# A two-layer trunk of attention and expert mixing on one core: other weight strips are kept on chip

## What is computed

```python
for layer in range(DEPTH):
    hn = rms_norm(h, ln_mix[layer])
    mix = gla_mixer(...) if layer % 2 == 0 else swa_mixer(...)   # linear attention / window of 128
    h = h + mix
    h = h + peer_ffn(rms_norm(h, ln_ffn[layer]), ...)
# peer_ffn, for each token: 8 heads, each picks 16 of 16384 experts
q = (xb @ w_q).reshape(BLK, PEER_HEADS, PEER_QDIM)      # scores against two sets of 128 keys
...
ue = u[e]                                                # e: top 16 of each set, top 16 of their sums
ve = v[e]
a = gelu(einsum('thkd,td->thk', ue, xb)) * g
return einsum('thk,thkd->td', a, ve)
```

## Time and profile before

| | |
|---|---|
| median of 3 runs | 2906.79 us (2900.58 to 2907.41) |
| the profiled execution | 2907.78 us, its span 2906.0 us |
| TensorE, VectorE, ScalarE, GpSimd busy | 78%, 75%, 41%, 43% of the span |
| mean granted TensorE clock | 0.921 |
| bytes moved by DMA | 1170.26 MB, 403 GB/s over the span |

### The profile page before, as it was taken

One profiled execution on the slowest core, in us unless ns is written; L12 is line 12 of the kernel. 1 busy time (PEld: TensorE's weight loads), 2 busy tenths in 40 slices (PEclk: granted clock), 3 DMA queues, 4 the chain that ended last, 5 costly groups with the idle time before them and its releaser, 6 DMA issues.

```text
span 2906.0 us, 27009 instructions
## 1 busy us (share of the span) xinstructions
PE 2257.9 (78%) x7300; PEld 1200.6 (41%) x7300; DVE 2185.6 (75%) x5166; ACT 1183.3 (41%) x3457; POOL 1263.8 (43%) x1049
## 2 busy tenths in 40 slices
PE   8678777687877877787787878878778777876667
PEld 6535443354423544243343434433444434432222
DVE  2687768875878757796688876988679876887664
ACT  2144324343443433344444463445534453433333
POOL 0155335443454433444434543354434454345555
PEclk9799899999998998899898998999899998998989
DMA  6499999999999999999999999999999999999998
GB/s 270 174 410 421 413 359 420 421 420 413 404 420 422 420 389 415 421 422 421 421 391 416 422 421 421 388 413 421 421 418 398 420 421 420 404 420 422 421 422 351
DMA packets 170816, 1170.26 MB, mean 403 GB/s; under 512 B 19668, under 2 KB 19928, under 8 KB 36136
## 3 DMA queue, kind: packets, MB, share of 16 engines
q0 software_dynamic: 147456, 1073.81, 89.4%
q1 hardware_dynamic: 23208, 94.74, 8.3%
HBM read 1164.28 MB, written 4.19 MB: 402 GB/s over the span
## 4 chain that ended last, share of the span: by engine, by line
DMA 29%; DVE 14%; PE 10%; issue 6%; POOL 3%; ACT 3%; POOLq 0%; DVEq 0%; ACTq 0%
DMA ring<-in_uv,pick 27%; PE acc L1716 5%; DVE ring L1093 5%; POOL ring L666 3%; PE ps L1511 3%; DVE side L1084 1%; DMA xc<-h 1%; DMA stream<-in_strips 1%; ACT diag L1369 1%; DVE arena L968 1%; DVE arena L949 1%; DVE arena L950 1%; ACT coef L1361 1%; DVE arena L1039 1%; DVE arena L1043 1%
## 5 line engine op out<-in xcount | busy, mean ns | idle before, releaser
L666 POOL DMA_INDIRECT ring<-in_uv,pick x1024 | 1259.3, 1230 | 1616.5 <-PE acc L1716 1084.1
L1716 PE MATMUL acc<-ring,diag 128*128 128x512 f32 x2988 | 1523.6, 652 | 474.6 <-ACT diag L1369 474.1
L1093 DVE CUSTOM_DVE_ANT_0 ring<-ring,h_now 128x1024 f32<-128x1024 f32 x1024 | 1236.0, 1223 | 494.5 <-DMA ring<-in_uv,pick 483.2
L1716 PEld LDWEIGHTS acc<-ring,diag 128*128 128x128 f32 x2988 | 576.0, 204 | 1286.0 <-ACT diag L1369 719.4
L1358 ACT ACTIVATE gelu<-dots 128x1 f32<-128x1 f32 x1024 | 206.1, 201 | 1263.2 <-DVE dots L1093 1261.8
L1084 DVE SCALAR_TENSOR_TENSOR side<-ring,coef,side 128x1024 f32<-128x1024 f32 x270 | 346.1, 1282 | 18.9 <-ACT coef L1361 18.9
L1361 ACT ACTIVATE coef<-gate,gelu 128x1 f32<-128x1 f32 x1024 | 301.9, 295 | 33.2
L1369 ACT ACTIVATE diag<-ident,coef 128x128 f32<-128x128 f32 x747 | 300.1, 402 | 28.2 <-PE acc L1716 3.9
L1511 PE MATMUL ps<-resident,actT 128*128 128x256 f32 x896 | 217.5, 399 | 16.5 <-ACT actT L1170 16.5
L1511 PEld LDWEIGHTS ps<-resident,actT 128*128 128x128 f32 x896 | 175.7, 200 | 59.4 <-ACT actT L1170 18.1
L1478 PE MATMUL ps<-actT,stream 128*128 128x128 f32 x960 | 125.6, 292 | 27.4 <-DMA stream<-in_strips 26.6
(11 more groups left out here) (196 smaller groups left out, 1439.2 us busy)
## 6 DMA issues: line engine op xcount, KB each, us to landing
stream<-in_strips SPq DMA_DIRECT2D x102, 512.0 KB, 9.3
resident<-in_strips SPq DMA_DIRECT2D x18, 1024.0 KB, 12.3
ring<-in_uv,pick POOLq DMA_INDIRECT x1024, 14.9
ring<-in_strips SPq DMA_DIRECT2D x9, 1024.0 KB, 19.7
arena<-in_keys SPq DMA_DIRECT2D x8, 512.0 KB, 7.8
xc<-in_x SPq DMA_DIRECT2D x4, 512.0 KB, 6.2
h<-arena SPq DMA_DIRECT2D x4, 512.0 KB, 11.5
xc<-h SPq DMA_DIRECT2D x4, 512.0 KB, 7.8
```

The source lines that it names most:

```text
L666: pool.indirect_dma_start(ring[:, n % SLOTS, :], None, tables[layer], bass.IndirectOffsetOnAxis(ap=pick[:, col:col + 1], axis=0),).then_in ...
L1093: dve.tensor_tensor_reduce(ring[:, slot, 0:D], ring[:, slot, 0:D], h_now[:], 1.0, 0.0, ALU.mult, ALU.add, dots[:, slot:slot + 1]).then_inc ...
L1716: m = pe.matmul(acc[:, b * 512:(b + 1) * 512], diag[:, turn % 4, :], ring[:, slot, D + b * 512:D + (b + 1) * 512], start=(r == 0 and i == ...
```

## The change

The nine kept strips are no longer the first nine of a layer. In layer 0 strips 5, 7, 9, 11, 13, 15, 16, 17, 18 are kept and 0 to 4, 6, 8, 10, 12, 14, 19 streamed; in layer 1 only 0, 4, 5 and 12 are streamed. Their number is as before. `left` now waits for the halves of its strip and says when it is done with them. q1, k0 and k1 of stage 0 stand at beats 41, 45 and 49. SP's queue is reordered to fit: the gain before strip 14 (layer 0) or 12 (layer 1), the keys behind all streamed strips, the rest of layer 1's kept strips behind three streamed ones, four kept strips loaded ahead in stage 2, not five. In the opening strips are loaded in the order of their numbers (14 and 19 last) into ring or `resident`, and all ring slots are free before the first gather, so that its wait for one goes.

```diff
-STREAMED = tuple(s - RESIDENT for s in STRIPS)
+KEPT = ((5, 7, 9, 11, 13, 15, 16, 17, 18), (1, 2, 3, 6, 7, 8, 9, 10, 11))
+PASSING = tuple(tuple(n for n in range(STRIPS[layer]) if n not in KEPT[layer]) for layer in range(2))
+STREAMED = tuple(len(p) for p in PASSING)
...
-SAYS = ({11: "r", 15: "y", 16: "pq0", 17: "pq1", 18: "pq2", 19: "pq3"},
-        {8: "y", 9: "pq0", 10: "pq1", 11: "pq2", 12: "pq3"})
-DONE = [[SAYS[layer].get(n) for n in range(RESIDENT, STRIPS[layer])] for layer in range(2)]
+SAYS = ({1: "q", 3: "k", 19: "pq3"}, {4: "kv", 12: "pq3"})
+DONE = [[SAYS[layer].get(n) for n in PASSING[layer]] for layer in range(2)]
 FREED = [[e for event in events for e in [None] * (CUTS - 1) + [event]] for events in DONE]
-GAIN_AT = (13 - RESIDENT, 10 - RESIDENT)
-AHEAD, AHEAD_AT, REST_AT = 5, 10, 5
-KEYS_AT = (16 - RESIDENT, 10 - RESIDENT)
+GAIN_AT = (PASSING[0].index(14), PASSING[1].index(12))
+AHEAD, AHEAD_AT, REST_AT = 4, 10, 5
...
-        "pe": {"hT": 34, "q0": 37, "q1": 39, "k0": 43, "k1": 46, "v0": 54, "v1": 54, "v2": 60, "v3": 60, "attn": 61,
+        "pe": {"hT": 34, "q0": 37, "q1": 41, "k0": 45, "k1": 49, "v0": 54, "v1": 54, "v2": 60, "v3": 60, "attn": 61,
...
             def load_kept_ahead(prep):
 
-                said_by(sp, "pe", before(prep), "v")
+                said_by(sp, "pe", before(prep), "r")
...
             def load_streamed(prep):
-                if prep.layer == 1:
-
-                    said_by(sp, "pe", prep, "o3")
-                    sp.dma_start(bias_out, b_out).then_inc(bias_loaded, 16)
                 opening = prep.first and prep.layer == 0
...
                 for n in range(STREAMED[prep.layer]):
-                    if n == GAIN_AT[prep.layer]:
+                    if n == GAIN_AT[prep.layer] + opening:
+
+                        if prep.layer == 1:
+                            if prep.first:
+                                load_kept_rest(prep)
+
+                            said_by(sp, "pe", prep, "o3")
+                            sp.dma_start(bias_out, b_out).then_inc(bias_loaded, 16)
 
                         said_by(sp, "pe", prep, "oT")
                         if prep.layer == 0:
 
                             said_by(sp, "dve", prep, "state1")
                         sp.dma_start(ffn_gain, gain_ffn[prep.layer:prep.layer + 1, :]).then_inc(gain_loaded, 16)
-                    if n == KEYS_AT[prep.layer]:
-
-                        said_by(sp, "pe", prep, "y")
-                        sp.dma_start(keysT, (keys0, keys1)[prep.layer]).then_inc(keys_loaded, 16)
...
+                said_by(sp, "pe", prep, "y")
+                sp.dma_start(keysT, (keys0, keys1)[prep.layer]).then_inc(keys_loaded, 16)
+
             def preps(prep, after):
-                if prep.first:
-                    load_kept_rest(prep)
                 load_streamed(prep)
...
+            def load_opening(begin, end):
+                for n in range(begin, end):
+                    if n in KEPT[0]:
+                        load_kept(Prep("gla", 0), KEPT[0].index(n))
+                    elif n in PASSING[0][:SLOTS]:
+                        i = PASSING[0].index(n)
+                        sp.dma_start(ring[:, i, :], strips[0][n]).then_inc(ring_loaded[i], 16)
...
-                    elif SAYS[0].get(RESIDENT + n, "r") not in ("r", "y", "pq0"):
-
-                        said_by(pool, "pe", Prep("gla", 0), SAYS[0][RESIDENT + n])
-                        alone(pool, passed["pool"])
...
-            def cut_done(n, c, ins):
-
-                if n >= RESIDENT and c < CUTS - 1:
+            def cut_done(prep, n, c, ins):
+
+                if passing(prep, n) and (c < CUTS - 1 or n not in SAYS[prep.layer]):
                     used_up(ins)
...
+                        if c == 0 and k % CUT == 0:
+                            cut_loaded(prep, n, k // CUT)
                         i = pe.matmul(ps[:, bank, (2 * side + c) * P:(2 * side + c + 1) * P],
                                       w[:, k, c * P:(c + 1) * P], actT[:, k, :], start=(k == 0),
                                       stop=(k == KT - 1))
+                        if c == 1 and k % CUT == CUT - 1:
+                            cut_done(prep, n, k // CUT, i)
```

42 lines of the change are left out of this document (19 added, 23 removed).

## The result

The changed kernel takes 2925.98 us (median; 2924.08 to 2929.37 over 4 runs), the kernel before 2906.26 beside it on the same chip. The ratio is 1.0069, 95% interval 1.0056 to 1.0083: slower by 20 us. The forecast was 2885 us with a range from 2870 to 2905, so the direction was wrong and the time lies outside the range. The profiled execution has a span of 2924.7 us.

What follows compares the result with a forecast made beforehand. DMA was taken as the bound wherever its ring is fed, at 421 GB/s. The sum was 2907.8 - 18.5 - 6 + 1 = 2884.3 us profiled, 2883.3 against the median, stated as 2885, range 2870 to 2905.

Steps and rivals of the forecast that it cites:

- Bytes: Whole kernel: as many strips streamed and kept per block as before, the 1170 MB unchanged, so 0 us.
- The pq strips of swa: Swa preparations: streaming only pq3 removes a 3.1 us wait at pq1; half taken, 1.5 a stage, 6 us won.
- Out and pq strips of gla: Gla preparations: all stream waits at out and pq go, winning 9.8 + 3.3 + 5.4 = 18.5 us of 22.1.
- Hand-overs of q and k: New streamed strips: 13 us each, leaving TensorE 2 us short in stage 0, inside the cover; 1 us lost.
- the slower rival: Hand-over of a q or k strip takes 17 us, not 13, deciding from about 15.5: 2915 us; chance 0.08.
- The 9.5: Stage 0: three beats and 2 us of waits put alpha 9.5 us later; VectorE may stand 0 to 2 us.
- the room of (b + 1) x 2.49: DMA time a hand-over b beats ahead has: b gathers and the strip itself, 2.49 us each.
- The rival on the clock: Stage 0: new waits drop TensorE's clock, 2.9 us more at each of seven hand-overs: 2895 us; chance 0.05.
- SP's queue, opening, stage starts: Reordered queue waits and loads, opening loads and the strip loaded at stage starts: 0 us each, opening at best 2.5.
- A rule beside the rows: DMA engines alternate between queues packet by packet, so a half strip takes 2.5 us; the sum used 11.3 us hand-overs instead.
- The signs: Right: stream waits gone at out and pq, DMA above 410 GB/s at 340 to 440 us; wrong: longer alpha wait.

Runs made afterwards that it cites:

- before's two profiles: The unchanged kernel before, profiled a first and a second time: gla loss 23.3 and 27.3 us, swa loss 18.8 and 20.6; the second execution took 2912.28 us.
- the mixed kernels: Three kernels against the kernel before: layer 1's strips as before, layer 0's exchanged so no two q or k strips stream consecutively; 2902.21, 2901.77 and 2902.42 us.

## Why the prediction was wrong

**The step that failed is "Bytes": "Nothing is added to or taken from the 1170 MB: 0 us."** The megabytes were the same, but three strips a swa stage were moved out of room that DMA had anyway, to places where it has none. That costs what the room held: swa loss 18.8 to 46.4, time +19 to +20, and it comes back when strips are put behind pq0 again (10 us for the first). I had the row in hand: the prediction says that VectorE is busy 36.1 of 40 us in the swa dips and that "most of these dips are top-k work", and concluded only that nothing is won there. If VectorE sets the pace in a dip, then what streams in it is free, and taking it away can't shorten the dip.

**The pq strips of swa, -6: wrong in sign.** The waits at pq1 did go. But they lay in a stretch whose length was VectorE's, so their removal gave nothing, and the dips grew by 28 us, nearly the strips' own 30.

**Out and pq strips of gla, -18.5: a third came.** (One reading behind it was wrong: of the four out strips of stage 2 only out1 and out3 start after a wait on the stream; out0 and out2 start with none, and out2 waits only for its second half.) The waits on the stream are gone, and VectorE's 15.0 us for y in stage 0 became 3.3, as forecast. Stage 2, forecast 5.4, gave 6.2 (6.7 to 0.5). Stage 1, forecast 3.3, gave 0.5 (4.7 to 4.2). Stage 0, forecast 9.8, gave nothing (11.9 to 12.6). Altogether 6 of loss, and against before's two profiles 6 to 10; in time layer 0's change alone is 0 within 3 us.

**Hand-overs of q and k, 13 us each: mis-sized.** Three of the four take 15.4 to 15.9 and one 11.5, 58.3 us together where 3 x 12.45 and, for v0 at five beats, 14.9 are room for 52.3: a lag of 6.0 us, not 2. (The prediction counted v0's hand-over as tight too; with 14.9 us for it, the slower rival's lag at 17 us each is 15.7, not 18.) The average of 14.6 lies below the 15.5 from which the slower rival was to decide. It seems to have decided stage 0 all the same, though not as told: DMA stayed at 419 in 220 to 280 us, alpha came 20.6 us later (275.4 for 254.8) instead of 9.5, and most of the loss came after 340. The 9.5 left out a term: three strips now stream between q0 and k1, 7.5 us of DMA time that the room of (b + 1) x 2.49 counts and alpha's sum did not; with three beats (7.5) that leaves 5.6 for waits. Strips kept between them bring stage 0 to 6.3 to 7.7 us, and the time to 2902. The slower rival had the sign with this mechanism, 2915; but the slower result is layer 1's, which no rival named.

**The rival on the clock** was right in its mechanism: among the new waits the granted clock is 0.83 for 0.93; what that cost by itself no run shows. **SP's queue, opening, stage starts, 0:** the mixed kernels load strips in the opening and at the stage starts in this order, with the gain before strip 14, and are not slower. The keys behind all streamed strips and four strips ahead for five they don't share: the first is in the kernel with layer 0 alone (2905.4), the second only in kernels with layer 1's change, and no run took either singly in layer 0. The opening's loss (to 165 us) is 69.0 for 70.5.

**"A rule beside the rows"**: the turns between queues, by which a half strip would take an estimated 2.5 us (the Trainium skill, DMA: Bandwidth & Descriptors, Queues, rings and completion order), don't agree with this trace: a half strip took 7.7 us from issue to landing in stage 3, and a hand-over up to 15.9. The estimate took packets of one size; in the queues' rows above a gather's packet has 7.3 KB and a strip's 3.6, so that turns would leave the strip a third of 421 GB/s, some 3.7 us by the same estimate, and still half of what was measured. The sum that went by the rows was nearer, and still short.

**The signs.** Of those for right came: no stream wait at out and pq steps, y under 7 us, and DMA at 419 and 420 GB/s in 700 to 740 and 1020 to 1120 us. Not: 340 to 440 us stands at 384, not above 410, q1's wait is 4.2, and the swa dips are deeper (329, 317, 318 and 362 GB/s in the four stretches of the earlier trace rows that had 384, 361, 383 and 404). Of those for wrong came the longer wait for alpha.

**What stays open:** how the room answers to a shorter top-k, which no run had; what keeps a strip issued at 1464 us from helping when one at 1481 us does; why the losses of stage 0 and 1 that remain in the gla stages (6 and 2 to 5 us) don't answer to the place of strips; and why stage 0's loss was 7.7 with strip 12 behind pq1 and 9.8 to 12.6 in other kernels with the same layer 0. The profile with the 7.7 is of the fastest execution of its kernel (2911.2, the median 2916.0), so its losses are rather on the low side.

## What to carry to other kernels

In a kernel bound by DMA, ask of each transfer not only how many bytes, but in which stretch: a load that falls where another engine's chain has a fixed length is free while room is left there, and spreading the loads evenly takes it out of there. The test is a row of the DMA queues: if the bound stream (here the gathers) moves the same megabytes in the stretch in both kernels, at less than full rate, the difference is room. Not all of it was filled here: of 9 us a stage two strips took 5, and a third strip won next to nothing. And before a chain of hand-overs through one buffer is moved, take its price from the same kind of use; three of four strips that are read twice took 15.4 to 15.9 us, not 11.3.

## What the runs showed of the hardware

A strip of 1 MiB handed over through one buffer took 11.3 us where it is read once (stage 2 of the kernel before) and 11.5 to 15.9 where it is read twice (stage 0 of the changed kernel), against 2.49 us of DMA time: most of the 11.3 can pass between the issue and the landing of a half strip among gathers (7.7 us median for 512 KB in stage 3). And the room in a stretch fills with falling return, about 10, 7 and 2 us for the first, second and third strip, over four stages and to some 3 us each.
